# Encoder step on one core: w_out units, their splits, gate instructions and parameter loads at other places

## The reference

```python
z = rmsnorm(x, norm_g) @ w_in                  # 1024 -> 2312 columns
a_out = u * (masked W_s @ rmsnorm(gelu(v)))    # A: gating in blocks of 128 rows
b_out = softmax(q k^T, sinks) v                # B: window attention, 8 q heads, 2 kv heads
c_h, (C, n, m) = mlstm(q, k, v, logi, logf)    # C: 4 heads, a state carried from block to block
mixed = concat([a_out, b_out, sigmoid(c_o) * c_h])
x = x + mixed @ w_out                          # 1024 -> 1024
x = x + (gelu(conv(up)[:2816]) * conv(up)[2816:]) @ w_down, up = rmsnorm(x) @ w_up
```

## Time and profile before

| what | value |
|---|---|
| median of three runs | 2668.32 us |
| profiled execution | 2665.21 us |
| its span | 2663.4 us |
| TensorE busy | 2556.0 us (96%) |
| DVE, ScalarE, GpSimd busy | 1469.9, 824.6, 194.0 us |
| mean granted TensorE clock | 0.979 |
| zb load, issue to landing (median) | 5.5 us |
| w_in group load (median), w_out part (median) | 5.3 us, 2.9 us |

### The profile page before, as it was taken

How to read it: one execution, slowest core, us unless ns; L and a number is a source line. 1 busy time by engine, 2 the same in 40 slices (tenths; PEclk the granted TensorE clock), 3 DMA queues, 4 the chain that set the end, 5 groups by cost and what they waited for, 6 DMA issues and landing times. The chain is left out here.

```text
span 2663.4 us, 42906 instructions
## 1 busy us (share of the span) xinstructions
PE 2556.0 (96%) x17027; PEld 2486.6 (93%) x17027; DVE 1469.9 (55%) x2779; ACT 824.6 (31%) x1497; POOL 194.0 (7%) x294
## 2 busy tenths in 40 slices
PE   8899988899999999999998999899999999999998
PEld 8899877899999999999998898788999999999998
DVE  3116677665555556555621267766655655555655
ACT  6224544432222222222323354444322212222224
POOL 0001112200000000000210011211000000000003
PEclk9999999999999999999999999899999999999999
DMA  4332322211111111110123233212111111111101
GB/s 145 119 125 90 105 84 62 67 56 48 41 48 43 46 48 33 47 48 24 34 68 127 102 108 114 68 46 90 47 42 49 40 49 40 49 40 48 48 9 69
DMA packets 196895, 170.82 MB, mean 64 GB/s; under 512 B 11062, under 2 KB 186452, under 8 KB 194516
## 3 DMA queue, kind: packets, MB, share of 16 engines
q1 hardware_dynamic: 196692, 167.95, 20.1%
HBM read 142.36 MB, written 25.55 MB: 63 GB/s over the span
## 5 line engine op out<-in xcount | busy, mean ns | idle before, releaser
L278 PE MATMUL bank<-actH,wb 128*128 128x384 f32 (+1 forms) x1472 | 496.1, 337 | 2.1 <-issue 2.1
L279 PE MATMUL bank<-actL,wb 128*128 128x384 f32 (+1 forms) x1472 | 490.9, 333 | 0.0
L280 PE MATMUL bank<-actH,wb 128*128 128x384 f32 (+1 forms) x1472 | 490.7, 333 | 0.0
L278 PE MATMUL bank<-wzH,actH 128*128 128x256 f32 (+3 forms) x1296 | 373.2, 288 | 20.3 <-ACT zst L1138 16.0
L1579 DVE TENSOR_TENSOR xT<-bank,xT 128x384 f32<-128x384 f32 (+1 forms) x576 | 288.3, 531 | 162.7 <-PE bank L280 162.3
L280 PE MATMUL bank<-wzH,actL 128*128 128x256 f32 (+3 forms) x1296 | 367.7, 284 | 0.0
L279 PE MATMUL bank<-wzL,actH 128*128 128x256 f32 (+3 forms) x1296 | 367.6, 284 | 0.0
L278 PE MATMUL bank<-actH,wHa 128*128 128x384 f32 (+1 forms) x992 | 326.6, 329 | 6.2 <-DVE upb L1828 6.2
L279 PE MATMUL bank<-actL,wHa 128*128 128x384 f32 (+1 forms) x992 | 326.0, 329 | 0.0
L280 PE MATMUL bank<-actH,wLa 128*128 128x384 f32 (+1 forms) x992 | 325.0, 328 | 0.0
L1355 ACT ACTIVATE cv<-upb,convc 128x1090 f32<-128x1090 f32 x88 | 114.4, 1300 | 560.9 <-DVE upb L1841 560.9
(11 more groups left out here) (253 smaller groups left out, 4104.4 us busy)
## 6 DMA issues: line engine op xcount, KB each, us to landing
raw<-in_w_up SPq DMA_DIRECT2D x88, 512.0 KB, 3.9
rawz<-in_w_in SPq DMA_DIRECT2D x22, 1024.0 KB, 5.3
raw<-in_w_down SPq DMA_DIRECT2D x44, 512.0 KB, 3.2
zb<-z_scratch SPq DMA_DIRECT2D x16, 1156.0 KB, 5.5
z_scratch<-zst SPq DMA_DIRECT2D x128, 128.0 KB, 1.8
raw<-in_w_out SPq DMA_DIRECT2D x128, 128.0 KB, 2.9
xin<-in_x_prompt SPq DMA_DIRECT2D x8, 512.0 KB, 7.9
out_y_prompt<-yst SPq DMA_DIRECT2D x8, 512.0 KB, 3.9
```

Source lines behind the costliest of these rows:

```text
L278: pe.matmul(out, aH, bH, start=first, stop=False)
L279: pe.matmul(out, aH, bL, start=False, stop=False)
L280: return pe.matmul(out, aL, bH, start=False, stop=last)
```

## The change

- Mixer parameters: `load_mixers` is cut in nine parts, one behind each of the z stores 18 to 26; the load of w_in group 3 is issued behind store 17, ahead of them.
- Order of z units 43 to 52: tile 0 of groups 7 and 8 comes first. Units from 49 on use banks 4 and 5. Tile 0 is loaded behind store 47, tile 1 behind store 50; the first block's TensorE part waits for evacuation 48.
- w_out units: (3, 7), and in blocks 4 to 8 j = 1 (ahead of A), 2 (behind the mix) and 7 (ahead of h's transposes). `W_HIGH`, `SQUARES` and `ADDS` are placed anew, the norm sum of chunk 0 moves from (6, 1) to (7, 2).
- The low parts of w_out's weights move from DVE to GpSimd, k = 12 to 15 in the tail too.
- ScalarE: the gate's log-sigmoid moves from `front_early` to behind j = 5 (`front_gate`); the output gate moves from the block's start to the end of the block before (`out_gate`). DVE's `front_early` moves behind the pT copies.

```diff
+        ZB = 49
+        Z_TAIL = ((7, 0), (7, 1), (8, 0), (7, 2), (8, 1), (7, 3), (8, 2), (7, 4), (8, 3), (8, 4))
...
+            elif u < Z1 - 10:
+                s, t = 2 + (u - 18) // 5, (u - 18) % 5
             elif u < Z1:
-                s, t = 2 + (u - 18) // 5, (u - 18) % 5
+                s, t = Z_TAIL[u - Z1 + 10]
...
+        def z_bank(u):
+            return u % 4 if u < ZB else 4 + u % 2
...
-        W_AT = {(3, 5): 0, (4, 0): 1, (4, 2): 2, (4, 5): 3, (5, 0): 4, (5, 2): 5, (5, 3): 6, (5, 5): 7, (6, 2): 8, (6, 4): 9,
-                (6, 6): 10, (7, 0): 11, (7, 3): 12, (7, 5): 13, (8, 0): 14, (8, 2): 15}
+        W_AT = {(b, j): 3 * b - 11 + (1, 2, 7).index(j) for b in range(4, NTOK) for j in (1, 2, 7)}
+        W_AT[3, 7] = 0
...
+        W_HIGH = {(3, 1): 0, (3, 2): 1, (3, 6): 2, (4, 1): 3, (4, 2): 4, (4, 6): 5, (5, 2): 6, (5, 6): 7, (6, 6): 8, (7, 2): 9,
+                  (7, 4): 10, (7, 6): 11}
+        W_LOW = {(3, 0): (0, 1), (3, 1): (2,), (4, 0): (3, 4), (4, 1): (5,), (5, 0): (6,), (5, 1): (7,), (6, 1): (8,),
+                 (7, 0): (9, 10), (7, 1): (11,)}
+        SQUARES = {(4, 1): (0, 0), (4, 3): (0, 1), (4, 5): (0, 2), (5, 1): (0, 3), (5, 3): (0, 4), (5, 5): (0, 5),
+                   (6, 1): (0, 6), (6, 3): (0, 7), (7, 3): (1, 0), (7, 4): (1, 1), (7, 5): (1, 2), (8, 0): (1, 3),
+                   (8, 1): (1, 4), (8, 3): (1, 5), (8, 4): (1, 6)}
+        ADDS = {(4, 1): (0, 1, 3), (5, 0): (0, 3, 4), (5, 1): (0, 4, 6), (6, 0): (0, 6, 7), (6, 1): (0, 7, 8),
+                (7, 1): (1, 1, 3), (8, 0): (1, 3, 5), (8, 1): (1, 5, 7)}
...
-                def load_mixers():
+                def load_mixers(part):
...
-                    z_stored(sp, l, 48 + i if i < 5 else 72 + i)
+                    z_stored(sp, l, (45, 47, 49, 51, 52)[i] if i < 5 else 72 + i)
...
                     if u == 17:
-                        load_mixers()
                         next_wz(3)
+                    if 18 <= u < 27:
+                        load_mixers(u - 18)
...
-                    if u == Z1 - 2:
+                    if u == 47:
                         load_zb(0)
-                load_zb(1)
+                    if u == 50:
+                        load_zb(1)
...
-                    elif u < Z1:
+                    elif u < ZB + 2:
                         pe.wait_ge(z_ev, l * ZU + u - 3)
...
-                    if v == 8:
+                    if v == 12:
                         pe.wait_ge(ms_r, ms_at(2 * l + 1, 0))
...
-                    if (b, j) == (6, 1):
-                        pe.wait_ge(bank_free, M0 + 7)
+                    if (b, j) == (7, 2):
+                        pe.wait_ge(bank_free, M0 + 11)
                         norm_sum(pe, 2 * l + 1, 0)
...
+                def front_gate(nx):
...
                     act.wait_ge(S["ax_r"], b1)
                     act.activation(ax[0:r], ax[0:r], ACT.Exp, scale=-1.0).then_inc(S["ax_e"], 1)
...
+                def out_gate(nx):
...
+                    wait(act, S["hc_r"], b1 - 1)
+                    act.activation(eo[0:r], z[0:r, C_O:C_O + 256], ACT.Exp, scale=-1.0).then_inc(S["eo_e"], 1)
...
                     dense(i, 5)
                     if nx is not None:
+                        front_gate(nx)
                         front_late(nx)
...
                     dense(i, 7)
+                    if nx is not None:
+                        out_gate(nx)
                     act.wait_ge(S["hT_r"], b1)
...
-                act.wait_ge(bank_free, M0 + WU)
+                norm_square(act, n, 1, 3, M0 + WU, 7)
...
+                def split_out(k):
+                    slot = 2 + k % 4 if k < 12 else k - 12 if k < 14 else k - 8
+                    pool.wait_ge(wo_h, l * N_WO + k + 1)
+                    pool.tensor_tensor(low(slot), raw(k % 2), high(slot).bitcast(F32), ALU.subtract).then_inc(wo_l, 1)
...
+                    if (b, late) in W_LOW:
+                        for k in W_LOW[b, late]:
+                            split_out(k)
...
+                norm_add(pool, n, 1, 7)
+                split_out(12)
+                split_out(13)
                 norm_power(pool, n, 1)
                 for m in range(1, KT):
                     norm_add(pool, n, 2, m)
+                    if m < 3:
+                        split_out(13 + m)
...
-                    if nx is not None:
-                        front_early(nx, link)
                     for c in range(nch):
...
                     if nch == 1:
                         dense(i, 4)
+                    if nx is not None:
+                        front_early(nx, link)
```

More of the change, by code:

```diff
@@ L501, in _ @@
                 M0 = l * MMS
-                def load_mixers():
[L505 to L531, removed]
-                                 I["state_C"][l, 0].rearrange("h v k -> v h k")).then_inc(par_in, 16)
-                    sp.dma_start(stin[HD:HD + 1, :], I["state_n"][l, 0:1].rearrange("o h k -> o (h k)")).then_inc(par_in, 16)
@@ L596, in _ @@
                         load_out(1)
-                load_out(2)
-                load_out(3)
+                for k in range(2, 5):
+                    load_out(k)
                 load_zb(5)
-                for k in range(4, 8):
+                for k in range(5, 8):
                     load_out(k)
@@ L725, in z_products @@
                         pe.wait_ge(act_l, (q0 + u // 6 + 1) * KT)
-                    out = bank[u % 4 if u < Z1 else 4 + u % 2][0:r, 0:w]
+                    out = bank[z_bank(u)][0:r, 0:w]
                     for k in range(KT):
@@ L951, in mixer @@
                     if b is None:
-                        pe.wait_ge(z_ev, l * ZU + Z1)
+                        pe.wait_ge(z_ev, l * ZU + ZB)
                         front_a(nx)
@@ L1137, in evac_z @@
                     act.wait_ge(rt_r, norm_at(2 * l, t // 3) + 1)
-                    act.activation(zst[0:r, u % 3, 0:w], bank[u % 4 if u < Z1 else 4 + u % 2][0:r, 0:w],
+                    act.activation(zst[0:r, u % 3, 0:w], bank[z_bank(u)][0:r, 0:w],
                                    ACT.Gelu if u < 18 else ACT.Copy, scale=rt[0:r, t:t + 1]).then_inc(z_ev, 1)
@@ L1186, in dense @@
                     if (b, j) in W_HIGH:
-                        for k in W_HIGH[b, j]:
-                            split_out(k)
+                        split_out(W_HIGH[b, j])
                     if (b, j) in SQUARES:
@@ L1209, in front_early @@
                                    z[0:r, B_Q:B_Q + 512].rearrange("t (v p d) -> t p v d", p=4, v=2), ACT.Copy).then_inc(S["qp_r"], 1)
+                def front_gate(nx):
+                    par, i, zi, r, kind = nx
+                    b1 = l * 9 + i + 1
                     act.wait_ge(S["ax_r"], b1)
@@ L1238, in front_late @@
                                        ACT.Copy).then_inc(cn_r, 1)
+                def out_gate(nx):
+                    par, i, zi, r, kind = nx
+                    b1 = l * 9 + i + 1
+                    z = zb[par]
+                    wait(act, S["hc_r"], b1 - 1)
+                    act.activation(eo[0:r], z[0:r, C_O:C_O + 256], ACT.Exp, scale=-1.0).then_inc(S["eo_e"], 1)
+                    act.wait_ge(S["eo_e"], b1)
+                    act.activation(eo[0:r], eo[0:r], ACT.Ln, bias=1.0).then_inc(S["eo_l"], 1)
+                    act.wait_ge(S["eo_l"], b1)
+                    act.activation(eo[0:r], eo[0:r], ACT.Exp, scale=-1.0).then_inc(S["eo_r"], 1)
                 def back(b, nx):
@@ L1448, in adds @@
                             norm_add(pool, 2 * l + 1, c, q)
-                    if (b, late) == (6, 1):
+                    if (b, late) in W_LOW:
+                        for k in W_LOW[b, late]:
+                            split_out(k)
+                    if (b, late) == (7, 1):
                         norm_power(pool, 2 * l + 1, 0)
@@ L1579, in add_x @@
                     dve.tensor_tensor(xT[:, m, t0:t0 + w], bank[b][:, 0:w], xT[:, m, t0:t0 + w], ALU.add).then_inc(bank_free, 1)
-                def split_out(k):
-                    dve.wait_ge(wo_h, l * N_WO + k + 1)
-                    slot = 2 + k % 4 if k < 12 else k - 12 if k < 14 else k - 8
-                    dve.tensor_tensor(low(slot), raw(k % 2), high(slot).bitcast(F32), ALU.subtract).then_inc(wo_l, 1)
                 def dense(b, j):
```

63 lines of the change are left out of this document (40 added, 23 removed).

## The result

The changed kernel takes 2602.01 us (median of 4 runs, 2601.21 to 2604.4) against 2668.41 us, a ratio of 0.975 with an interval of 0.9734 to 0.9767. That is 66.4 us less; 2592 was forecast, with a range of 2572 to 2624. The profiled execution is the slowest of the four: 2604.4 us, with a span of 2602.6 against 2663.4 before, 60.8 less.

What follows compares the result with a forecast made beforehand. TensorE, busy 96% of the span, was taken as the bound, so only its waits and half clock could be won. Gains 21.1+10.3+45.4 = 76.8 us off 2665.2 gave 2588.4, as a median 2592 (range 2572 to 2624).

Steps and rivals of the forecast that it cites:

- R1: Rival, middle of mixer blocks: VectorE and GpSimd bind, moved units leave matmuls uncovered; 22 us a layer stay; 2611 us, 25%.
- (a): Parameter loads in the z stage: w_in group 3's load queued behind them stalls TensorE and lowers its clock; gain 21.1 us.
- (b): First mixer block, behind z unit 52: loading tile 0 early starts the dense matmuls sooner; gain 10.3 us.
- (c): Mixer blocks 3 to 8: waits and half clock lose 35.0 us a layer, 12.3 would stay; gain 45.4 us.
- one fall of the clock 1.5: Within (c): half-clock time left after the change, 1.5 us a layer.
- 2.0 a block: Within (c), blocks 4 to 7: waits left, 1.2 us on WT, 0.5 on L905, 0.3 on A.
- R2: Rival, mixer: GpSimd's splits fall beside PSUM readers and ScalarE keeps up; 5 us a layer stay; 2577 us, 11%.
- The gates, priced at nothing: Gate reordering: costs nothing in blocks 0 to 2 while z units cover it, otherwise 0.2 us for each.
- The tail, priced at nothing: Behind the mixer: low parts 12 to 15 on GpSimd come some 4 us later, yet TensorE gets no wait.
- R4: Rival, slower: each of 16 splits a layer stalls VectorE and TensorE for its full length, 43.5 us; 2687 us, 4%.
- R3: Rival, z stage: (a) only moves, through late evacuation 18 or lagging z stores; 21.1 us not gained; 2613 us, 7%.
- R5: Rival: the gates or the loads add a wait of their own that eats all gains; 2668 us, 2%.

## Why the prediction was right, and where it was off

The sign and the range held. By the profiled execution 76.8 us were forecast and 60.8 came; by medians the forecast lies 10.5 us under the result. The result is 10 us from the forecast and 9 from rival R1's 2611, so the number alone does not choose between them. By the prediction's own signs (a) and (b) came as forecast, the longest split took 2.74 us and no unit waited for wo_l; but blocks 4 and 5 took 34.6 and 31.5 us in layer 1, over the 31 that was to show it wrong.

**(a), 21.1 us.** Right: the swap alone gave 20.3, its undoing took 18.0. The step named the late w_in load and it was that; the careful count of SyncE's issues behind each store was idle work.

**(b), 10.3 us.** Right as far as it was seen: what the z part saved beyond (a)'s 10.1 a layer is 4.4 and 6.9, against 4.8 and 5.5. The first dense matmul behind unit 52 came after one wait, 1.05 us for qp. It was not undone by itself.

**(c), 45.4 us forecast, 31.1 found.** This is the term that was mis-sized, and in it the clock. I left 12.3 us a layer, 10.8 of waits and 1.5 of half clock. Layer 0 between the marks, in the changed kernel and in the one with the early low parts on VectorE:

```profile
289.65:465.27 175.62, 163.05 (x1173) 141.18 (x1172) 145.98 (x359) 80.88 (x245) 68.25 (x75) 0.96 0.25 77
```

```profile
290.01:452.94 162.93, 156.39 (x1173) 137.38 (x1171) 133.45 (x371) 80.30 (x245) 39.92 (x63) 1.00 0.28 83
```

TensorE is idle for 12.6 us in layer 0 and 10.3 in layer 1, near the 10.8. The same matmuls keep it busy for 163.1 us where full clock needs 156.4: 6.7 us at half clock in layer 0 and 6.4 in layer 1, where 1.5 was put. The failed step is "one fall of the clock 1.5", and ahead of it the even "2.0 a block". The mechanism was in the text: "A split can thus hold a DVE instruction up to 2.7 us", in the middle, where "There is no slack"; the split's length was right too (2.42 us in the blocks, 2.58 and 2.72 behind them). But the waits were spread evenly, one split at a time. Block 4 has two splits in a row and VectorE four multiplies in a row, so 1.01 us became 5.48 and one wait 3.1 us; blocks 4 to 7 of layer 1 are idle 3.1, 2.9, 1.2 and 1.8 us, and in blocks 4 and 5 the granted clock is 0.85 and 0.95. With the splits out of the way, 26.9 us were won in each layer (low parts on VectorE), or 26.6 and 27.6 (behind rv), more than the 22.7 forecast; so 163 us for blocks 3 to 8 is what the new places of the units allow, some 7 us over the full-clock work, near rival R2's 5.

How much the clock takes is not fixed: in the profiles of the three runs with the same instructions in these blocks (the last four low parts, the parameters behind and ahead of the load) (c) is worth 35.9, 36.4 and 41.3 us. The 31.1 is the lowest of four, and all stay under 45.4.

**The gates, priced at nothing.** Wrong, and hidden by the sum: with the old order the measured 2639.6 lies outside the range of 2572 to 2624, so that the forecast held is in part luck. I priced the order only in blocks 0 to 2 and let the L905 waits vanish with the moved units. The order alone was worth 12.5 us, and taking it out of the changed kernel costs 37.6. Without it the six mixer blocks take 192.9 us, no less than before: moving the units, with the low parts at these places on GpSimd, wins nothing by itself, and the 28.8 us that are left of the gain are about (a) and (b). It is that combination: with the old order and the low parts on VectorE the blocks take 173.5 us, so the units' places alone do win.

**The tail, priced at nothing.** Wrong by 2.0 us in the profile, and its undoing gave some 6.5: I looked at when the four low parts are wanted, not at VectorE's low parts of the norm (L384) beside them.

**Rivals.** R1 named the right waits (PT and WT) with a size of 22 us a layer, where 19.2 and 16.7 stayed over the full-clock work; its cause, units moved away, was not enough: with the units at the same places and the splits elsewhere, 163 us. R4's price per split held for VectorE: 31 of the 32 splits in the trace stopped an instruction, which then took 1.95 to 2.84 us. Yet the kernel is not slower, as TensorE waited for few of them: it was idle for 12.6 and 10.3 us in blocks 3 to 8, where R4 had 43.5 us a layer for the splits alone. R3 and R5 fell.

## What to carry to other kernels

A split on GpSimd costs nothing or several us, by what VectorE has in that stretch: put it beside instructions that read PSUM and outside the chain, or leave it where it was. Price the order of small instructions ahead of a copy that TensorE needs by what the first of them waits for, not by their 0.2 us. And where one queue issues small loads and a large one that is wanted soon, try the swap before anything that spreads.

## What the hardware showed that was not expected

A VectorE instruction of four columns took 2.07 us and one of 192 columns 2.47 us beside GpSimd instructions of 2.4 us, and in a row of four, two waited for one each. Readers of PSUM that met a split lost nothing: mixA from a bank 0.41 us in three cases, and pT copies 0.68 and 0.69 us as elsewhere. And a short wait lowered the clock: the text held that 1.3 us had not done so elsewhere, but in the changed kernel's tail a wait of 0.97 us for acc, with 0.81 us of one-column matmuls behind it, was followed by half clock. In layer 0 a wait of 1.45 us at the same place was too, while 1.8 us in block 4 with the early low parts on VectorE was not. What decides it stays open.

```profile
1782.00:1784.00 2.00, 1.43 (x9) 1.33 (x10) 1.90 (x3) 2.00 (x4) 0.39 (x1) 1.00 0.84 250
1784.00:1786.00 2.00, 2.00 (x9) 2.00 (x8) 2.00 (x5) 2.00 (x5) 0.00 (x0) 0.54 0.11 17
```
